# A two-layer transformer block on one core: the low half of each weight unit written over its loaded data, four such buffers and three high halves, and a block compression with stationary and moving operand exchanged

## The reference, cut to what matters

```python
def compress(kv, pe, w1, w2):
    # block i covers tokens [i*16, i*16+32)
    blocks = blocks + pe[None, None, :, None, :]
    flat = blocks.transpose(0, 1, 3, 2, 4).reshape(b, n_cmp, g, CMP_BLOCK * d)
    return jax.nn.silu(flat @ w1) @ w2

k_cmp = rmsnorm(compress(kc, cmp_pe_k, cmp_w1_k, cmp_w2_k), k_norm_g)
v_cmp = compress(vc, cmp_pe_v, cmp_w1_v, cmp_w2_v)
```

## Time and profile before

| | |
|---|---|
| median of three runs | 2690.52 us (2689.93 to 2702.18) |
| profiled execution, its own time | 2692.48 us |
| its span from first to last instruction | 2690.7 us |
| TensorE busy in matmuls | 2540.4 us, 94% of the span |
| VectorE, ScalarE, GpSimd busy | 1351.4, 1045.0, 176.6 us |
| granted TensorE clock, mean | 0.965 of full speed |
| read from HBM | 217.79 MB |

### The profile page before, as it was taken

The page is one execution under the profiler, slowest core; times in us unless marked ns, Lnnn a source line. Parts: engine busy times, 40 slices in busy tenths (PEclk is TensorE's granted clock), DMA queues, the critical chain, the costliest instruction groups (busy, mean ns, idle before and its releaser), DMA issues.

```text
span 2690.7 us, 31535 instructions
## 1 busy us (share of the span) xinstructions
PE 2540.4 (94%) x12154; PEld 2110.2 (78%) x12154; DVE 1351.4 (50%) x2707; ACT 1045.0 (39%) x1865; POOL 176.6 (7%) x236
## 2 busy tenths in 40 slices
PE   8999998899999999999999999999989988899998
PEld 6887877787878787877888887877877776788886
DVE  5435445333465656676443445555544455543444
ACT  4323334234454554444322233655632345322232
POOL 0000000000111111210000000211100002000000
PEclk9999999898999999999999999999989999999999
DMA  3454343122212111113223233211112331223322
GB/s 133 112 131 117 104 132 118 55 79 71 79 56 71 55 63 55 63 63 102 89 91 103 94 88 128 71 56 56 56 47 89 107 118 55 72 96 91 102 87 85
DMA packets 86094, 231.38 MB, mean 86 GB/s; under 512 B 8456, under 2 KB 23432, under 8 KB 85946
## 3 DMA queue, kind: packets, MB, share of 16 engines
q1 hardware_dynamic: 78480, 217.18, 24.8%
q10 hardware_dynamic: 7466, 12.19, 2.5%
HBM read 217.79 MB, written 11.53 MB: 85 GB/s over the span
## 4 chain that ended last, share of the span: by engine, by line
PE 82%; DVE 9%; ACT 5%; issue 2%; POOL 1%; ACTq 1%; DMA 0%; DVEq 0%; SPq 0%
PE bank L874 80%; DVE t_wlo L1710 2%; PE bank L1041 2%; ACT t_whi L1330 1%; DVE t_tmp L1782 1%; DVE t_ss L1911 1%; POOL t_pp L2265 0%; ACT t_pp L1459 0%; DVE t_CB L1782 0%; POOL t_pw L2267 0%; DVE t_tmp L1752 0%; DVE t_ST L2160 0%; ACT L1343 0%; ACTq L1400 0%; ACT t_tmp L1330 0%
## 5 line engine op out<-in xcount | busy, mean ns | idle before, releaser
L874 PE MATMUL bank<-t_XH,t_whi 128*128 128x512 f32 x2064 | 829.2, 402 | 53.1 <-DVE t_wlo L1710 25.0
L874 PE MATMUL bank<-t_XH,t_wlo 128*128 128x512 f32 x2064 | 815.2, 395 | 0.0
L874 PE MATMUL bank<-t_XL,t_whi 128*128 128x512 f32 x2064 | 815.0, 395 | 0.0
L1710 DVE TENSOR_TENSOR t_wlo<-t_raw,t_whi 128x1024 fp32r<-128x1024 f32 (+2 forms) x412 | 472.2, 1147 | 463.9 <-ACT t_whi L1330 458.8
L1330 ACT ACTIVATE t_whi<-t_raw 128x1024 fp32r<-128x1024 f32 (+2 forms) x412 | 407.9, 991 | 393.2 <-PE bank L874 379.1
L874 PEld LDWEIGHTS bank<-t_XH,t_whi 128*128 128x128 f32 x2064 | 395.7, 192 | 148.4 <-issue 42.3
L874 PEld LDWEIGHTS bank<-t_XH,t_wlo 128*128 128x128 f32 x2064 | 394.2, 191 | 85.5
L874 PEld LDWEIGHTS bank<-t_XL,t_whi 128*128 128x128 f32 x2064 | 395.6, 192 | 79.0
L874 PE MATMUL bank<-t_RX,t_whi 128*128 128x512 f32 x1056 | 331.6, 395 | 0.0
L1782 DVE TENSOR_TENSOR t_tmp<-bank,t_RB 128x512 f32<-128x512 f32 x170 | 117.1, 689 | 263.0 <-PE bank L874 260.7
L874 PEld LDWEIGHTS bank<-t_RX,t_whi 128*128 128x128 f32 x1056 | 198.2, 188 | 48.0
(11 more groups left out here) (300 smaller groups left out, 2886.1 us busy)
## 6 DMA issues: line engine op xcount, KB each, us to landing
t_raw<-in_f_in SPq DMA_DIRECT2D x88, 512.0 KB, 3.3
t_raw<-in_f_out SPq DMA_DIRECT2D x32, 384.0 KB, 3.1
t_raw<-in_w_merge SPq DMA_DIRECT2D x24, 512.0 KB, 3.2
t_raw<-in_w_conv SPq DMA_DIRECT2D x24, 512.0 KB, 3.2
t_raw<-in_fg SPq DMA_DIRECT2D x22, 512.0 KB, 3.2
t_raw<-in_fu SPq DMA_DIRECT2D x22, 512.0 KB, 3.2
t_raw<-in_f_out SPq DMA_DIRECT2D x32, 320.0 KB, 2.9
t_raw<-in_w_g SPq DMA_DIRECT2D x16, 512.0 KB, 3.2
```

The costliest lines, as they stand in the source:

```text
L874: return e.matmul(o, l, r, start=start, stop=stop, skip_group_check=True)
L1710: e.tensor_tensor(wlo[n % NW][:, 0:width], raw[n % NRAW][:, 0:width], f32(whi[n % NW][:, 0:width]), ALU.subtract).then_inc(*w_lo.tick(n))
```

## The change

1. The buffers `raw` become four, and `wlo` of a unit lies at the same addresses as its `raw`: VectorE writes the remainder over the loaded data. `whi` becomes three. The whole takes seven buffers, as before.
2. ScalarE's `split(n)` waits for TensorE's unit n - 3, VectorE's only for `whi`. `load(n)` waits until TensorE is through with unit n - 4. The splits are issued up to two units behind that of an item.
3. Every unit is split now, those of the compression too. There the windows become stationary (124 columns) and the weights moving (256 columns, three float32r matmuls for each slice). VectorE makes the windows' halves ahead of it (`cround`: four instructions for the high halves with the embedding added, four for the low ones, in one of two buffers). One bank instead of two collects the result, ScalarE applies Silu to `HS`, TensorE turns it over with two transposes (`hturn`), and VectorE copies it to `hid`.
4. `order()` issues `cround(q, j)` one step ahead of `cmp(q, j)`, which takes one more step for each q and so moves later jobs among the tiles.
5. At the start four loads are mixed with those of x, not three.

```diff
-NW = 2
-NRAW = 3
+NHI = 3
+NRAW = 4
...
             for j in range(4):
-                w.lin("cmp", q, j, name="cmp_w1", j=4 * q + j, split=False)
+                w.add("cround", q, j)
+                if j:
+                    w.lin("cmp", q, j - 1, name="cmp_w1", j=4 * q + j - 1)
                 yield
+            w.lin("cmp", q, 3, name="cmp_w1", j=4 * q + 3)
+            yield
+            w.add("hturn", q)
...
-    raw = [sb(f"raw{i}", [P, UNIT]) for i in range(NRAW)]
-    whi = [sb(f"whi{i}", [P, UNIT], F32R) for i in range(NW)]
-    wlo = [sb(f"wlo{i}", [P, UNIT], F32R) for i in range(NW)]
+    raw = [place(f"raw{i}", ARENA + i * UNIT, UNIT) for i in range(NRAW)]
+    wlo = [place(f"wlo{i}", ARENA + i * UNIT, UNIT, F32R) for i in range(NRAW)]
+    whi = [sb(f"whi{i}", [P, UNIT], F32R) for i in range(NHI)]
...
         def cmp(q, j, n):
-            if j == 0:
-                for ht in range(2):
-                    take("d", ("cmp", q, ht), True)
-                on.wait_ge(*evac.at(("c2", q, 1)))
-            bs = [banks[("cmp", q, ht)] for ht in range(2)]
-            on.wait_ge(*d_raw[n % NRAW].at(n))
+            b = take("d", ("cmp", q), True) if j == 0 else banks[("cmp", q)]
+            hi, lo = weights(n)
+            on.wait_ge(*x_lo.at(("cround", q, j)))
+            h, l = CH[0][j % 2], CH[1][j % 2]
             for kk in range(4):
...
+                c = slice(kk * 256, (kk + 1) * 256)
+                f = three(b[0:124, 0:256], h[:, kk, 0:124], l[:, kk, 0:124], hi[:, c], lo[:, c],
+                          j == 0 and kk == 0, j == 3 and kk == 3)
...
+        def hturn(q):
+            b = take("d", ("hturn", q))
+            on.wait_ge(*curve.at(("hs", q)))
+            for ht in range(2):
+                f = e.transpose(b[:, ht * P:ht * P + 124], HS[0:124, ht * P:(ht + 1) * P], ident[0:124, 0:124])
+            f.then_inc(*full.tick(("hturn", q)))
...
         def split(n):
             width = unit[n][2]
-            if unit[n][4]:
-                on.wait_ge(*d_raw[n % NRAW].at(n))
-                on.wait_ge(*full.at(("u", n - NW)))
-                copy(whi[n % NW][:, 0:width], raw[n % NRAW][:, 0:width]).then_inc(*w_hi.tick(n))
+            on.wait_ge(*d_raw[n % NRAW].at(n))
+            on.wait_ge(*full.at(("u", n - NHI)))
+            copy(whi[n % NHI][:, 0:width], raw[n % NRAW][:, 0:width]).then_inc(*w_hi.tick(n))
...
-            while n < min(upto - 1 + NW, len(unit)):
+            while n < min(upto - 1 + NHI, len(unit)):
                 split(n)
...
+        def cround(q, j):
+            h, l = CH[0][j % 2], CH[1][j % 2]
+            on.wait_ge(*evac.at(("c2", q, 1)))
+            on.wait_ge(*full.at(("cmp", q, j - 2) if j > 1 else ("cmp", q - 1, j + 2)))
+            src = [C2[:, :, 2 * kt:2 * kt + 481:16] for kt in range(4 * j, 4 * j + 4)]
+            for kk in range(4):
+                o = h[:, kk, 0:124].rearrange("p (g c) -> p g c", g=4)
+                e.tensor_scalar(o, src[kk], v(("pek", "pev")[q], 4 * j + kk), None, ALU.add).then_inc(*calc.tick(("cround", q, j)))
+            on.wait_ge(*calc.at(("cround", q, j)))
+            for kk in range(4):
+                o, i = (x[:, kk, 0:124].rearrange("p (g c) -> p g c", g=4) for x in (l, h))
+                e.scalar_tensor_tensor(o, src[kk], v(("pek", "pev")[q], 4 * j + kk), f32(i), ALU.add, ALU.subtract).then_inc(
+                    *x_lo.tick(("cround", q, j)))
...
         def load(n):
-            if n >= NRAW:
-                if unit[n - NRAW][4]:
-                    on.wait_ge(*w_lo.at(n - NRAW))
-                else:
-                    on.wait_ge(*full.at(("u", n - NRAW)))
+            on.wait_ge(*full.at(("u", n - NRAW)))
...
-            while n < min(upto - 1 + NW + NRAW, len(unit)):
+            while n < min(upto + NRAW, len(unit)):
```

More of the change, by code:

```diff
@@ L184, in add, with unit @@
         self.items.append((item, len(self.units)))
-    def unit(self, name, j, width=UNIT, off=0, split=True):
-        self.units.append((name, j, width, off, split))
+    def unit(self, name, j, width=UNIT, off=0):
+        self.units.append((name, j, width, off))
         return len(self.units) - 1
@@ L729, in build @@
     hid = [place(f"hid{q}", 24576 + q * 256, 256).rearrange("p (t g c) -> p t g c", t=2, g=4) for q in range(2)]
+    CH = [[place(f"CH{q}{d}", 25728 + 1024 * q + 512 * d, 512, F32R).rearrange("p (k n) -> p k n", k=4) for d in range(2)]
+          for q in range(2)]
+    HS = place("HS", 27776, 256)
     KX = place("KX", 25088, 128)
@@ L1472, in cmp @@
         def cmp(q, j, n):
-            for ht in range(2 if j == 3 else 0):
-                on.wait_ge(*evac.at(("hb", q, ht)))
-                o = banks[("cmp", q, ht)][:, 0:124].rearrange("p (g c) -> p g c", g=4)
-                on.wait_ge(*cleared.at("hid"))
-                e.activation(hid[q][:, ht, :, 0:31], o, ACT.Silu, bias=hb[:, 2 * q + ht:2 * q + ht + 1]).then_inc(
-                    *curve.tick(("hid", q, ht), ("free", ("cmp", q, ht))))
+            if j == 3:
+                on.wait_ge(*full.at(("cmp", q, 3)))
+                on.wait_ge(*full.at(("hturn", q - 1)))
+                e.activation(HS[0:124, :], banks[("cmp", q)][0:124, 0:256], ACT.Silu).then_inc(
+                    *curve.tick(("hs", q), ("free", ("cmp", q))))
         def scaled_sq(b, sq, x, gain, sq_item, x_item, free):
@@ L1706, in split @@
             width = unit[n][2]
[L1707 to L1711 removed]
+            on.wait_ge(*w_hi.at(n))
+            e.tensor_tensor(wlo[n % NRAW][:, 0:width], raw[n % NRAW][:, 0:width], f32(whi[n % NHI][:, 0:width]),
+                            ALU.subtract).then_inc(*w_lo.tick(n))
         def low(o, x, hi, item, *more):
@@ L1945, in kvc, with hturn @@
                     *evac.tick(("c2", q, x), ("free", ("kvc", q, x))))
-        def cmp(q, j, n):
-            if j == 3:
-                on.wait_ge(*full.at(("cmp", q)))
-                for ht in range(2):
-                    e.tensor_copy(hb[:, 2 * q + ht:2 * q + ht + 1], banks[("cmp", q, ht)][:, 126:127]).then_inc(
-                        *evac.tick(("hb", q, ht)))
+        def cround(q, j):
[11 more added lines that the diff above has]
+                    *x_lo.tick(("cround", q, j)))
+        def hturn(q):
+            on.wait_ge(*full.at(("hturn", q)))
+            on.wait_ge(*cleared.at("hid"))
+            src = banks[("hturn", q)][:, 0:256].rearrange("p (t n) -> p t n", t=2)
+            for ht in range(2):
+                e.tensor_copy(hid[q][:, ht, :, 0:31], src[:, ht, 0:124].rearrange("p (g c) -> p g c", g=4)).then_inc(
+                    *evac.tick(("hid", q), ("free", ("hturn", q))))
         def kc2():
```

36 lines of the change are left out of this document (12 added, 24 removed).

## The result

The changed kernel takes 2627.51 us (median of four runs, 2622.03 to 2628.84), the kernel before beside it 2694.72 us. The ratio is 0.9746, 95% interval 0.9725 to 0.9767. The profiled execution took 2628.84 us, its span 2627.0. The prediction said 2632, worked out from a kernel before of 2690.5 us; the fourth run of that kernel, taken beside the changed one, moved its median to 2694.7.

A forecast was written before the change was run, and what follows sets the result against it. TensorE was taken to bound the kernel: its matmuls, pauses and half-clock stretches. Lookahead -37, compression -24.3, start +2.6 and loads 0 gave -58.7 us on a span of 2690.7, a median of about 2632 us, range 2612 to 2658.

The forecast's parts named there:

- The likeliest case: Whole kernel: the forecast of about 2632 us, own range 2615 to 2655, chance 0.68.
- A: Lookahead, at TensorE's waits for `t_wlo`: earlier splits remove nearly all waits and the half-clock stretches behind them, -37 us.
- C: Start: the second unit's split stands ahead of the first norm copy and delays the first matmul, +2.6 us.
- B: Compression in the memory attention: shorter units and less half clock, against new waits, -24.3 us.
- 41 us at half clock: Six half-clock stretches between 508 and 631 us, beginning or continuing in `cmp` units; their reduction counted as -11.6 us.
- The new waits: Compression: TensorE waits for work standing behind `cround` on VectorE, +11.5 us, bounds nothing to 24.
- Rival 2: Compression: it brings nothing, as score tiles hang on VectorE's chain; the 24.3 us stay away, 2656 us, chance 0.12.
- The rounding's price: `cround` on VectorE: eight instructions reading every 16th element, 366 ns each, 2.9 us for eight.
- D: Loads: issued at most some 3 us later, but with one unit more of time ahead, 0 us.
- rival 3: Short units: late loads hold up ScalarE's splits and tile work, 50 us, about 2682 us, chance 0.05.
- room of 5.7 us: Short units: time a load may take before TensorE feels it, against 3.2 us median and 7.8 at most.

The follow-up runs named there:

- the buffers alone: The kernel before with the changed kernel's buffers, lookahead and loads, its compression left as it was: 2650.35 us, ratio 0.9837.
- the doubled rounding: The changed kernel with the eight instructions of each `cround` run twice on VectorE: 2644.81 us, ratio 0.9813.
- B alone: The changed kernel with the old buffers, loads and lookahead, so only the new compression is left: 2679.37 us, ratio 0.9952.
- the mended start: The changed kernel, but items ahead of the first unit bring only its own split: 2624.88 us, one run.

## Why the prediction was right, and which terms were off

**The sum.** -58.7 us were forecast, -67 measured (2694.72 to 2627.51, and again 2693.0 to 2625.63). The likeliest case came. That the sum is so near is in part luck: its two parts were A with C at -34.4 and B at -24.3 us, and each alone measured -44 and -15. They were off by 9 us in opposite directions, and the 8 us more came from having both.

**A, the lookahead: right in its mechanism, too small by some 10 us.** The waits of 34 us are gone, as is the wait view's row. That late issue and not lack of time or of buffers made them is shown by the kernel that differs only in the issue. The term that was too small is "A = -34 + 2 - 5": of the 34 us none stayed, and the measured effect with C in it is -44 us (median) or -50 us (profiled).

The traces show where these 50 us come from. The kernel before and the one with the buffers alone issue the same 12154 matmul instructions in the same order, so the steps from start to start can be subtracted one by one. The 29 waits named `t_wlo` give 34.6 us, as forecast. Another 7.0 us are late splits which the wait view calls `t_sn` or issue, and which the forecast left out: three before, of 3.63, 3.21 and 2.31 us at 396.48, 1656.91 and 2300.64, less a new one of 2.51. One of them:

```profile
1655.54 1.23 DVE L1710 TENSOR_TENSOR t_wlo<-t_raw,t_whi 128x1024 fp32r<-128x1024 f32 x1 [2.00 <-ACT t_whi L1330]
...
1656.91 0.76 PE L874 MATMUL bank<-t_XH,t_whi 128*128 128x512 f32 x1 [3.21 <-DVE t_sn L1726]
```

The matmul doesn't read `t_sn`; its low half was ready at 1656.77. The clock gives 10.3 us where I had 5: the time at half clock fell from 191 to 172 us. Intervals without a shown pause give 3.6. Against this stand 1.8 at the start and 3.7 of waits for `t_XL` and `t_rn` that grew. That is 34.6 + 7.0 + 10.3 + 3.6 - 1.8 - 3.7 = 50.0. Between the profiled execution and the median of that kernel lie 8 us, and the mean clock differs with them (0.968 against 0.964 to 0.966).

**B, the compression: right where A is given.** From the buffers alone (2650.35) to the whole change (2627.51) it is -23 us; -24.3 were forecast. The two profiled executions differ by 14 us only, since that of the buffers alone was a fast one; within 494 to 681 us of the table they differ by 25.8. Most pieces can be read above. The unit takes 1.44 us. An `hturn` takes 0.14 us from start to start (two transposes, 608.28 us), not 0.45, and its wait did not come. Of the 41 us at half clock 27 are gone, where I had counted on 30: from the first unit to behind the last there are four stretches of 3.41 us. The score of tile 4 waited 1.12 + 1.82 = 2.94 us (forecast 2.9), that of tile 12 1.84 + 1.46 = 3.30 (forecast 3.3), `cmp 1 3` 1.85 (forecast 2.2). `cmp 0 0` waited 0.41, not 1.2, and `cmp 1 1` not at all. Instead the squares for the next queries (`t_tmp`, L1856) were waited for 2.63 and 2.83 us. Before, the timeline of TensorE has for the same two:

```profile
551.27 1.05 PE L874 MATMUL bank<-t_cst,t_tmp 128*128 128x1 f32 x8 [1.53 <-DVE t_tmp L1851]
...
609.34 1.05 PE L874 MATMUL bank<-t_cst,t_tmp 128*128 128x1 f32 x8 [1.53 <-DVE t_tmp L1851]
```

That is 2.4 us that no step had named. The new waits together are 0.41 + 2.94 + 3.30 + 1.85 + 2.4 = 10.9 us. The forecast's pieces, 1.2, 2.9, 3.3, 1.2, 2.2 and 0.5, make 11.3 and not the 11.5 it wrote. Rival 2, that VectorE's chain eats all of it, is wrong as to its sum, but the doubled rounding shows how near it is: 17 of 19.7 us more on VectorE were seen.

**The step that was missing: A and B are not independent.** The sum took them apart, and with both in place it comes out. But B alone brings 15 us and not 24, since its new work makes the late splits later (42.1 against 29.3 us of waits), and the lookahead is then worth 59 us (from 2686 to 2627) or 52 (from 2679), where it was worth 44 without B and 34 were forecast with C. Whoever had built the compression first would have called it a small gain.

**The rounding's price.** 366 ns an instruction were taken; they measured 325 and 422 ns, each started 0.26 and 0.36 us behind the one before, 2.5 us for a `cround` instead of 2.9. The Trainium skill, "Advanced Engine Details and Errata", section "SBUF Cachelines", says that accesses which each touch a different 16-byte line pay a penalty. The trace agrees: without the step the same instructions take 279 and 344 ns. It was no reason against the change, as it costs 4 us of VectorE in all.

**C, the start: +2.6 forecast, 2.9 measured at the first matmul,** and 2.5 given back by the mended start.

**D, the loads: right on TensorE, wrong on ScalarE.** I expected few waits of ScalarE for loads behind the start. Its view after has these (us in total, times, longest):

```profile
ACT t_whi L1338 <- DMA t_raw<-in_f_out: 21.2, 5, 6.5
ACT t_whi L1338 <- DMA t_raw<-in_f_in: 11.3, 4, 4.7
ACT t_whi L1338 <- DMA t_raw<-in_fg: 3.9, 1, 3.9
ACT t_whi L1338 <- DMA t_raw<-in_fd: 3.0, 1, 3.0
```

With the smaller rows 43 us in 14 waits, where before there was the one of 4.27 us at the start; 6 us of the 43 in two waits are the start here too. The splits now run so far ahead that they meet the loads. 22.8 us of it, in six waits, lie between 152 and 195 us, in feed-forward 1, where TensorE has no pause, and no wait of TensorE is one for these splits, so the 0 holds. The mechanism of rival 3 is there, but not in its place, the short units from 2083 us (3.0 us in two waits), and the usual landing stayed at 3.2 us. (Its room of 5.7 us is three units of 2.9 less 0.4 and 2.6; the forecast wrote two.) How much room is left before it shows was not tried.

## What to carry to other kernels

When the engines that prepare operands are half idle and the consumer still waits, look at the place in the program where the preparation is issued: a third high half and a fourth buffer did nothing until the issue ran one unit further ahead, and then gave 59 us. Look behind the names of a wait view too: a late operand can be booked on another signal that came at the same time. Pack the moving operand and sum ahead of the product what else takes matmuls of a single column (in float32r this took the unit from 4.95 to 2.62 us), let the wide side move (2.62 to 1.44), and try float32 as it is before splitting it. Cost two parts of a change also together, when both use the same engine's slack.

## What was not expected of the hardware

- Eight instructions of a float32 matmul with 124 stationary and 256 moving packed columns took 1.54 us, the same product with the weights stationary and 124 strided moving columns, and the embedding's single columns, 4.95 us in 32 instructions. How much of this is the step, the single columns or the sides was not run apart.
- Runs of one kernel on one chip differ by 5 to 13 us, and that goes with TensorE's mean granted clock: the buffers alone ran in 2642.36 us at 0.968 and in 2652.12 us at 0.964. That is 2.4 us for one thousandth of the mean clock, so differences of a few us need several runs.
- Behind the start the changed kernel and the one with the mended start have the same instructions, and yet their distance in the table goes 1.2 us, 4.0 and 1.6 at 494, 797 and 1645 us. Small differences between two traces inside such stretches say nothing on the kernels.
